# A hybrid encoder trunk in fp32 on one core: one merged form for all residual norms, layer 0's adaLN on TensorE, and a new order in the attention's tail

## The chip, the cores and the metric

One core of a Trainium2 chip. The metric is the device time of one execution in microseconds. The engines are TensorE (PE), VectorE (DVE), ScalarE (ACT), GpSimd (POOL) and SyncE (SP), which issues the DMAs.

## What is computed

The sequence has 512 positions of 1024 channels. Layer 0 mixes with a diagonal state space (S5) that ends in a GLU, layer 1 with differential attention; each is followed by a gated FFN with a short convolution. Around every sub-layer stands the same frame, with shift, scale and gate from a conditioning vector (adaLN):

```python
mod = cond @ ada_w[i] + ada_b[i]
sh_t, sc_t, g_t, sh_c, sc_c, g_c = jnp.split(mod, 6, axis=-1)
h = modulate(rms_norm(x, norm_g[i, 0]), sh_t, sc_t)
h = s5_mixer(h, ...)        # or diff_attention(h, ...)
x = x + g_t[:, None, :] * rms_norm(h, norm_g[i, 1])
h = modulate(rms_norm(x, norm_g[i, 2]), sh_c, sc_c)
h = conv_ffn(h, ffn_w_in[i], ffn_conv_w[i], ffn_conv_b[i], ffn_w_out[i])
x = x + g_c[:, None, :] * rms_norm(h, norm_g[i, 3])
```

So between two sub-layers stand two root mean squares: that of the sub-layer's output y, and that of the new x.

## The kernel before

All engines run hand-written programs tied by semaphores. Activations lie transposed, channels on partitions: x is 8 tiles of 128 channels by 512 positions (`f` counts tiles). Weights come in units of 1 MB (128 x 2048) through two buffers `raw`; ACT makes the high part `whi`, DVE the low part `wlo` (`split_high`, `split_low`), and a product is three matmuls per step, high by high, high by low, low by high (`gemm_step`, L1738 to L1740). A unit has 16 steps: two output tiles (halves) of eight `k`.

**adaLN.** `ada_w` comes as 48 units of 1 MB. Of layer 0 the first third (8 units) is made by PE in the start-up (`ada_unit`, L1615: four matmuls of one column by 512 a unit, all to partition 0), copied by ACT to one row and turned into a column by PE (L1636). The other 40 units are summed by DVE (`ada_step`, L1250) beside the GLU (two a unit) and the first FFN (two in each of the first twelve units), and PE turns the sums with ones (`reduce_acc`, L1622).

**Start-up.** DVE makes the S5 matrices (`complex_rows`), PE transposes them (L1646), DVE normalises u, PE spreads its modulation (L1650, for which DVE waits before `output_powers`, L1100 to L1105), and four pieces of scan and Toeplitz products (L1679) follow.

**The merge.** Behind the GLU DVE and PE work in two rounds (`first_norms`, `statistic`): squares of y, root, y times gate times root, x plus that; then squares of the new x, root, and the next input with high and low part. Behind FFN 0 and behind the output projection they use one round (`tile_sums`, `both_roots`, `next_input(r)`, `barrier(r)`, r = 1, 2): for each tile, when it is ready, the sums of y*y, x*y*gate and (y*gate)^2 are added, and the new x's mean square follows from these and the old one, which is kept in `stat[:, 24:28]`. PE keeps itself busy there with idle products (L1778). DVE writes the new input tile by tile, and the first FFN unit follows it.

**Attention's tail.** Each head is done in four query blocks: scores (L1937), row maximum, exponentials, `combine` (L1492), `turn` (L1953), `weigh` (L1962). PE does these for a head while it does projection steps of another (`attend`, whose `fill` gives some steps at two places per block). The last two heads are filled by the first two units of the output projection (`early_output`, `wo_step`). Behind the last weighing stand `head_norm` on DVE, `turn_out` (L1971), the low part of the last head on POOL, and the rest of the projection; its third unit has its own buffers `wx`.

## Time and profile before

| what | value |
|---|---|
| median of 3 runs | 1386.8 us (1385.84 to 1389.02) |
| profiled execution | 1383.9 us |
| its span | 1382.1 us |
| PE busy | 1235.3 us (89%) |
| DVE, ACT, POOL busy | 860.7, 497.8, 430.3 us |
| chain that ended last | PE 75%, DVE 16%, issue 3%, DMA 2% |

The page gives the share of each engine and the span in slices. Busy time says little by itself: what counts is which wait ends last in a stage. The timeline lists instructions in order, with the idle time before them and what ended it in brackets. A float32 matmul shows as two records, a float32r one as one.

### The profile page before, as it was taken

What the parts mean: (1) busy time and instruction counts of PE and PEld (TensorE: products, weight loads), DVE (VectorE), ACT (ScalarE), POOL (GpSimd) and SP (SyncE); (2) the same over time, 40 slices, a digit from 0 to 9 for tenths busy, and PEclk for the clock granted to TensorE, in tenths of its full rate; (3) what the DMA queues carried; (4) which work ended last, traced back from release to release, by engine and by line L of the source; (5) the groups of instructions that cost most, each with busy time, mean ns of one, the idle gap of its engine ahead of it and who ended that gap; (6) DMA issues with size and microseconds to landing.
All of it is one profiled execution on the core that took longest, in us unless ns stands there. A gap on an engine that the chain in (4) does not pass through costs nothing.

```text
span 1382.1 us, 17492 instructions
## 1 busy us (share of the span) xinstructions
PE 1235.3 (89%) x6312; PEld 994.6 (72%) x6312; DVE 860.7 (62%) x1107; ACT 497.8 (36%) x749; POOL 430.3 (31%) x274
## 2 busy tenths in 40 slices
PE   5532599988999999999999999887999999999995
PEld 0222588876888888888878776666778888887884
DVE  8999878747989744424295468775964444443323
ACT  3052342224433433414233254544544434342311
POOL 3993011123554534300020443530133344431001
PEclk9766799958999999999999999999999999999998
DMA  8001988802767513233222332220122222323211
GB/s 343 1 1 25 167 265 309 299 31 74 291 245 289 196 64 110 101 104 110 92 73 92 92 92 62 75 77 32 61 92 91 91 91 98 114 92 110 104 61 61
DMA packets 35430, 164.97 MB, mean 119 GB/s; under 512 B 4528, under 2 KB 14000, under 8 KB 17200
## 3 DMA queue, kind: packets, MB, share of 16 engines
q1 hardware_dynamic: 34368, 163.97, 35.0%
q8 instruction: 35, 0.57, 0.2%
q10 hardware_dynamic: 1008, 0.27, 0.1%
q14 instruction: 19, 0.16, 0.0%
HBM read 156.95 MB, written 3.08 MB: 116 GB/s over the span
## 4 chain that ended last, share of the span: by engine, by line
PE 75%; DVE 16%; issue 3%; DMA 2%; ACT 1%; SPq 1%; POOL 1%; DVEq 0%; ACTq 0%; POOLq 0%
PE psum L1738 16%; PE psum L1739 16%; PE psum L1740 16%; PE psum L1879 5%; PE psum L1880 5%; PE psum L1881 5%; PE psum L1622 2%; PE psum L1962 1%; PE psum L1937 1%; PE psum L1823 1%; SPq L375 1%; PE psum L1922 1%; PE psum L1923 1%; PE psum L1924 1%; DVE ca L1103 1%
## 5 line engine op out<-in xcount | busy, mean ns | idle before, releaser
L1738 PE MATMUL psum<-hhi,whi 128*128 128x512 f32 x960 | 382.4, 398 | 3.9 <-DVE hlo L1309 2.7
L1739 PE MATMUL psum<-hlo,whi 128*128 128x512 f32 x960 | 376.8, 393 | 0.0
L1740 PE MATMUL psum<-hhi,wlo 128*128 128x512 f32 x960 | 376.7, 392 | 0.0
L1187 DVE TENSOR_TENSOR wlo<-raw,whi 128x2048 fp32r<-128x2048 f32 x82 | 199.0, 2427 | 169.6 <-ACT whi L693 169.6
L693 ACT ACTIVATE whi<-raw 128x2048 fp32r<-128x2048 f32 x81 | 155.1, 1915 | 178.1 <-PE psum L1881 146.1
L567 POOL TENSOR_TENSOR ca<-ca,cb 128x512 f32<-128x512 f32 x44 | 138.6, 3151 | 247.2 <-ACT ca L803 247.2
L1738 PEld LDWEIGHTS psum<-hhi,whi 128*128 128x128 f32 x960 | 182.0, 190 | 45.6 <-issue 5.5
L1740 PEld LDWEIGHTS psum<-hhi,wlo 128*128 128x128 f32 x960 | 181.9, 189 | 38.6
L1739 PEld LDWEIGHTS psum<-hlo,whi 128*128 128x128 f32 x960 | 182.1, 190 | 36.2
L1403 DVE SCALAR_TENSOR_TENSOR ca<-psum,convp,ca 128x511 f32<-128x511 f32 x44 | 32.9, 749 | 200.0 <-ACT ca L799 199.9
L1879 PE MATMUL psum<-ghi,whi 128*128 128x512 f32 x352 | 137.2, 390 | 1.5 <-DVE wlo L1187 1.5
L1880 PE MATMUL psum<-glo,whi 128*128 128x512 f32 x352 | 137.0, 389 | 0.0
L1881 PE MATMUL psum<-ghi,wlo 128*128 128x512 f32 x352 | 136.9, 389 | 0.0
L553 POOL TENSOR_TENSOR x<-x,y_late 128x512 f32<-128x512 f32 x17 | 22.9, 1351 | 293.2 <-DVE y_late L1366 172.0
L1250 DVE SCALAR_TENSOR_TENSOR ada_acc<-ada_ring,cond,ada_acc 128x2048 f32<-128x2048 f32 x40 | 106.1, 2652 | 3.0 <-DMA ada_ring<-in_ada_w 2.8
L799 ACT ACTIVATE ca<-psum,convp 128x512 f32<-128x512 f32 x44 | 34.2, 778 | 134.3 <-PE psum L1740 133.8
L569 POOL TENSOR_TENSOR glo<-ca,ghi 128x512 f32 x44 | 69.6, 1583 | 41.5 <-ACT ghi L805 41.5
L805 ACT ACTIVATE ghi<-ca 128x512 f32 (+1 forms) x44 | 27.8, 633 | 151.7 <-POOL ca L567 151.7
L1879 PEld LDWEIGHTS psum<-ghi,whi 128*128 128x128 f32 x352 | 66.1, 188 | 16.1 <-DVE wlo L1187 2.4
L1880 PEld LDWEIGHTS psum<-glo,whi 128*128 128x128 f32 x352 | 66.1, 188 | 13.7
L1881 PEld LDWEIGHTS psum<-ghi,wlo 128*128 128x128 f32 x352 | 66.1, 188 | 13.7
L873 ACT ACTIVATE prob<-psum,stat 128x128 f32<-128x128 f32 (+3 forms) x64 | 33.2, 523 | 75.9 <-DVE stat L1477 75.9
(344 smaller groups left out, 1736.0 us busy)
## 6 DMA issues: line engine op xcount, KB each, us to landing
raw<-in_units SPq DMA_DIRECT2D x92, 1024.0 KB, 4.8
ada_ring<-in_ada_w SPq DMA_DIRECT2D x40, 1024.0 KB, 4.8
ada_raw<-in_ada_w SPq DMA_DIRECT2D x8, 1024.0 KB, 14.9
toep<-toeplitz_rows SPq DMA_DIRECT2D x32, 128.0 KB, 8.6
qk_sw<-ca SPq DMA_DIRECT2D x32, 128.0 KB, 2.3
u<-in_x_blocks SPq DMA_DIRECT2D x1, 2048.0 KB, 14.1
x<-in_x_t SPq DMA_DIRECT2D x1, 2048.0 KB, 8.3
out_t<-x SPq DMA_DIRECT2D x8, 256.0 KB, 2.0
```

What stands on the lines that cost most here:

```text
L567: nc.gpsimd.tensor_tensor(ca[:, s, :], ca[:, s, :], cb[:, s, :], ALU.mult).then_inc(g_ready, 1)
L569: nc.gpsimd.tensor_tensor(glo[:, j, :], ca[:, s, :], ghi[:, j, :].bitcast(F32), ALU.subtract).then_inc(g_lo, 1)
L693: A(whi[:, s, :], raw[:, s, :], ACT.Copy).then_inc(split_hi, 1)
L799: A(dst[:, s, :], psum[:, 2 * s + i, :], ACT.Identity, scale=convp[:, layer, j, i, 2:3], bias=convp[:, layer, j, i, 3:4]).then_inc(tap2, 1)
L1187: TT(wlo[:, s, :], raw[:, s, :], whi[:, s, :].bitcast(F32), ALU.subtract).then_inc(split_lo, 1)
L1250: STT(ada_acc[:, slot, :], ada_ring[:, e, :], cond[:, 1, bass.ds(k[0], 1)], ada_acc[:, slot, :], ALU.mult, ALU.add).then_inc(ada_added, 1)
L1738: M(out, w_hi, hi[:, k, :], start=(k == 0), stop=False)
L1739: M(out, w_hi, lo[:, k, :], start=False, stop=False)
L1740: return M(out, w_lo, hi[:, k, :], start=False, stop=(k == KT - 1))
L1879: M(out, whi[:, s, w], ghi[:, row, :], start=(fixed and row == 0), stop=False)
L1880: M(out, whi[:, s, w], glo[:, row, :], start=False, stop=False)
L1881: return M(out, wlo[:, s, w], ghi[:, row, :], start=False, stop=(fixed and row == JT - 1))
```

## The change

It does three things.

1. The merge behind the GLU takes the form of the later two, as r = 0. The squares of x are made by ACT (`x_square`) and added by DVE (`x_square_add`) in the first four GLU units; PE sums them ahead of unit 7. Each GLU tile's sums are made in its unit (`glu_squares`, `tile_sums(0, f)`). The next unit's second buffer is split in halves, as it was behind the projection. POOL adds seven of the eight residual tiles instead of three.
2. The second and third third of layer 0's adaLN (16 units) move from DVE to PE's start-up, through two buffers; each unit's four matmuls now write partitions 0, 32, 64, 96 of one bank. The 24 units of layer 1 stay on DVE: one in each GLU unit, one or two in each of the first twelve FFN units.
3. In the tail the early projection steps are given out in halves, by counts per place, and eight of the third unit's sixteen steps go behind the last weighing.

```diff
-N_ADA_PE = KT
+N_ADA_PE = 3 * KT
...
-        POOL_X = ((1, 3, 5), tuple(range(1, KT)), tuple(range(1, KT)), (1, 3, 5))
+        POOL_X = 3 * (tuple(range(1, KT)),) + ((1, 3, 5),)
...
+            eng.wait_ge(h_low, KT * r + f + 1)
+        def ada0_slot(n):
+            return n % N_ADA0 if n < KT else n % 2
+        def ada0_count(n):
+            return 16 * (n // N_ADA0 + 1 if n < KT else (n - KT) // 2 + 3)
...
-                wait(sp, ada_used, n + 1 - N_ADA0)
-                sp.dma_start(ada0_raw[:, n % N_ADA0, :], a["ada_w"][n]).then_inc(ada0_landed[n % N_ADA0], 16)
+                wait(sp, ada_used, n + 1 - N_ADA0 if n < KT else n - 2 if n < KT + 2 else n - 1)
+                slot = ada0_slot(n)
+                sp.dma_start(ada0_raw[:, slot, :], a["ada_w"][n]).then_inc(ada0_landed[slot], 16)

...
+            load_unit(2, 0, None)
+            load_unit(3, 1, None)
+            def load_one(i, s, half):
+                load_ada(i + 2, s)
+                load_unit(i + 4, s, half)
+                load_ada(2 * i - 10, 0)
+                load_ada(2 * i - 9, 1)
+            pairs(sp, 0, N_GLU + 4, load_one)
+            pairs(sp, N_GLU + 4, N_GLU + 8, load_both)
+            for i in range(N_GLU + 8, N_GLU + 10):
+                load_ada(i + 6, i % 2)
+                load_unit(i + 4, i % 2, None)
...
+            def copy_row(third):
+
+                act.wait_ge(ada_used, KT * third + KT)
+                if third == 2:
+                    act.wait_ge(mod0_psum, 1)
+                for b in range(4):
+                    ins = A(sq[32 * b:32 * b + 1, third % 2, :], psum[32 * b:32 * b + 1, third % 2, :], ACT.Copy)
+                ins.then_inc(row_copied, 1)
+
...
+            def x_square(f):
+
+                act.wait_ge(x_in, 16)
+                wait(act, xsq_added, f - 2 if f > 2 else 0)
+                A(x_sq[:, f % 2, :] if f else x_sum[:], x[:, f, :], ACT.Square).then_inc(xsq_ready, 1)
+
+            def glu_squares(f):
+
+                y, g = y_glu[:, f, :], gate[:, 0, f:f + 1]
+                act.wait_ge(y_ready, f + 1)
+                wait(act, sum_a, f - 2 if f > 2 else 0)
+                A(sq[:, f % 2, :] if f else ssum[:], y, ACT.Square).then_inc(sqa_ready, 1)
+                wait(act, sum_c, f - 2 if f > 2 else 0)
+                A(glu_sq[:, f % 2, :] if f else cb[:, 1, :], y, ACT.Square, scale=g).then_inc(sqc_ready, 1)
+                act.wait_ge(sqc_ready, f + 1)
+                A(y, y, ACT.Copy, scale=g).then_inc(yg_ready, 1)
+
...
+            dve.wait_ge(mod_psum, 2)
+            modulation(0, (2, 3, 4, 5))
+            signal(mod_read)
...
+                    pairs(dve, 0, 4, partial(body, first=lambda j, s, half: ada_step(
+                        j + KT, s, half + KT // 2 + 1, j, 1)))
+                    dve.wait_ge(acc_clear, 3)
+                    pairs(dve, 4, 8, partial(
+                        body, first=lambda j, s, half: ada_step(2 * j + (KT - 4), 0, j + 3, j, 1),
+                        second=lambda j, s, half: ada_step(2 * j + (KT - 3), 1, j + 3, j - 4, 0)))
+                    pairs(dve, 8, 12, partial(body, first=lambda j, s, half: ada_step(
+                        j + (KT + 4), s, half + 7, j - 4, 0)))
...
+            def glu(i, s):
+                dve.wait_ge(sig_ready, i + 1)
+                TT(y_glu[:, i, :], psum[:, 2 * s, :], ca[:, s, :], ALU.mult).then_inc(y_ready, 1)
+                if i < N_GLU - 1:
+                    split_low(i + 2, s, None)
+                    if i < KT // 2:
+                        if i:
+                            x_square_add(2 * i)
+                        x_square_add(2 * i + 1)
+                    ada_step(i, s, i // 2 + 1, i, 0)
+                tile_sums(0, i)
+
+            for i in range(N_GLU - 1):
+                glu(i, i % 2)
+            first_half_low(0)
+            ada_step(N_GLU - 1, 1, 4, N_GLU - 1, 0)
+            glu(N_GLU - 1, 1)
+            next_input(0, {KT - 1: lambda: second_half_low(0)})
...
-            def ada_unit(k, s):
-
-                pe.wait_ge(ada0_landed[s], 16 * (k // N_ADA0) + 16)
+            def ada_unit(n):
+
+                third, k = divmod(n, KT)
+                pe.wait_ge(ada0_landed[ada0_slot(n)], ada0_count(n))
+                if k == 0:
+                    wait(pe, row_copied, third - 1)
-                    ins = M(psum[0:1, b, :], cond[:, 1, k:k + 1], ada0_raw[:, s, 512 * b:512 * b + 512],
+                    ins = M(psum[32 * b:32 * b + 1, third % 2, :], cond[:, 1, k:k + 1],
+                            ada0_raw[:, ada0_slot(n), 512 * b:512 * b + 512],
+
+            def turn_row(third):
+
+                pe.wait_ge(row_copied, third + 1)
+                if third:
+                    pe.wait_ge(mod_psum if third > 1 else mod0_psum, 1)
+                for b in range(4):
+                    rows = slice(32 * b, 32 * b + 1)
+                    for q in range(4):
+                        f = THIRD * third + 4 * b + q
+                        ins = M(psum[:, 7, f:f + 1], sq[rows, third % 2, P * q:P * q + P], ones[rows, 0:1],
+                                start=True, stop=True)
+                    if b < 3:
+                        ins.then_inc(row_turned, 1)
+                        pe.wait_ge(row_turned, 3 * third + b + 1)
+                ins.then_inc(mod_psum if third else mod0_psum, 1)
...
+                if t % 2:
+                    ada_unit(2 * KT + t // 2)
             pe.wait_ge(umod_rhs, 2)
...
+            pairs(pe, 2, N_GLU - 2, glu)
+            glu(N_GLU - 2, 0, None)
+            pe.wait_ge(xsq_added, KT - 1)
+            for t in range(QT):
+                ins = M(psum[:, 5, t:t + 1], x_sum[:, P * t:P * t + P], col[:, 0:1],
+                        start=True, stop=True)
+            ins.then_inc(stat_x, 1)
+            pe.wait_ge(y_ready, N_GLU - 2)
+            pe.wait_ge(split_lo, N_GLU)
+            for step in range(2 * KT):
+                ins = gemm_step(1, step, hhi, hlo)
+                if step == KT - 1:
+                    ins.then_inc(glu_half, 1)
+            ins.then_inc(unit_done, 1)
...
-            def early_output(steps_):
-
-                for m, k in steps_:
-                    if k == 0:
-                        pe.wait_ge(split_lo, U_WO + m + 1)
-                        pe.wait_ge(raw_copied, 2 * (HEADS - 1 + m))
-                    wo_step(m, k)
+            def early_output(steps_, counts):
+
+                todo = iter([(m, k, half) for m, k in steps_ for half in range(2)])
+                for count in counts:
+                    for m, k, half in itertools.islice(todo, count):
+                        if k == 0 and half == 0:
+                            pe.wait_ge(split_lo, U_WO + m + 1)
+                            pe.wait_ge(raw_copied, 2 * (HEADS - 1 + m))
+                        wo_step(m, k, half)
...
-            attend(HEADS - 2, 0, early_output([(0, k) for k in range(5)]))
-            attend(HEADS - 1, 1, early_output([(1, k) for k in range(5)] + [(0, 5), (1, 5)]))
+            attend(HEADS - 2, 0, early_output([(0, k) for k in range(5)], (1, 1, 1, 1, 1, 1, 2, 2)))
+            attend(HEADS - 1, 1, early_output([(1, k) for k in range(5)] + [(0, 5), (1, 5)],
+                                              (1, 1, 2, 2, 2, 2, 2, 2)))
             turn(HEADS - 1, 3)
             weigh(HEADS - 1, 3)
+            pe.wait_ge(split_lo, U_WO + 3)
+            pe.wait_ge(exp_done, 8 * HEADS)
+            for k in range(KT // 2):
+                for half in range(2):
+                    wo_step(2, k, half)
             turn_out(HEADS - 1)
 
             for m in range(2):
-                wo_step(m, KT - 2)
+                for half in range(2):
+                    wo_step(m, KT - 2, half)
             for m in range(2):
-                pe.wait_ge(ot_lo, KT + 2)
-                gemm_step(m, KT - 1, ohi, olo).then_inc(y_tile, 1)
-                gemm_step(m, 2 * KT - 1, ohi, olo).then_inc(unit_done, 1)
-            for m in range(2, N_WO):
-                pe.wait_ge(split_lo, U_WO + m + 1)
-                if m == 3:
-                    pe.wait_ge(sqc_ready, KT + 2)
-                w = (4, wx[:, 0], wx[:, 1]) if m == 2 else (0, None, None)
-                for step in range(2 * KT):
-                    ins = gemm_step(1, step, ohi, olo, *w)
-                    if step == KT - 1:
-                        ins.then_inc(y_tile, 1)
-                ins.then_inc(unit_done, 1)
+                wo_step(m, KT - 1, 0).then_inc(y_tile, 1)
+                wo_step(m, KT - 1, 1).then_inc(unit_done, 1)
+            for half in range(2):
+                for k in range(KT // 2, KT):
+                    ins = wo_step(2, k, half)
+                ins.then_inc(unit_done if half else y_tile, 1)
+            pe.wait_ge(split_lo, U_WO + 4)
+            pe.wait_ge(sqc_ready, 2 * KT + 2)
+            for step in range(2 * KT):
+                ins = gemm_step(1, step, ohi, olo, 0)
+                if step == KT - 1:
+                    ins.then_inc(y_tile, 1)
+            ins.then_inc(unit_done, 1)
```

The order of `ada_w` in memory (`_ada_units`) follows the new order of use.

PE in the start-up, around the transposes of `lb`. Before:

```order
L1615 MATMUL psum<-ada_raw,cond 1x512 [waits ada0_landed1]
L1615 MATMUL psum<-ada_raw,cond 1x512 x3
L1615 MATMUL psum<-ada_raw,cond 1x512 [waits ada0_landed2]
L1615 MATMUL psum<-ada_raw,cond 1x512 x3
L1636 MATMUL psum<-ones,mod_row 128x1 [waits row_copied]
L1636 MATMUL psum<-ones,mod_row 128x1 x15
L1646 MATMUL psum<-ident,lb_re 128x128 [waits row0_ready,lb_dve,lb_pool]
L1646 MATMUL psum<-ident,lb_re 128x128 x7
```

Now (unit 15 of `ada_raw`, the transposes, units 16 and 17):

```order
L1585 MATMUL psum<-ada_raw,cond 1x512 x3
L1631 MATMUL psum<-ident,lb_re 128x128 [waits row0_ready,lb_dve,lb_pool]
L1631 MATMUL psum<-ident,lb_re 128x128 x7
L1585 MATMUL psum<-ada_raw,cond 1x512 [waits row_copied,ada0_landed0]
L1585 MATMUL psum<-ada_raw,cond 1x512 x3
L1631 MATMUL psum<-ident,lb_re 128x128 [waits inb_ready]
L1631 MATMUL psum<-ident,lb_re 128x128 x3
L1631 MATMUL psum<-ident,lb_re 128x128 [waits inb_ready]
L1631 MATMUL psum<-ident,lb_re 128x128 x3
L1585 MATMUL psum<-ada_raw,cond 1x512 [waits ada0_landed1]
L1585 MATMUL psum<-ada_raw,cond 1x512 x3
L1631 MATMUL psum<-ident,lb_re 128x128 [waits inb_ready]
```

Units 8 to 15 stand ahead of the first transpose, and of the other eight one behind every eight transposes, each with the wait for its load.

DVE in the GLU, the last two units before the merge. Before:

```order
L1263 TENSOR_TENSOR y_glu<-psum,ca 128x512 [waits sig_ready]
L1250 SCALAR_TENSOR_TENSOR ada_acc<-ada_ring,cond,ada_acc 128x2048 [waits ada_added,ada_landed0]
L1187 TENSOR_TENSOR wlo<-raw,whi 128x2048 [waits split_hi]
L1250 SCALAR_TENSOR_TENSOR ada_acc<-ada_ring,cond,ada_acc 128x2048 [waits ada_added,ada_landed1]
L1263 TENSOR_TENSOR y_glu<-psum,ca 128x512 [waits sig_ready]
```

Now, the third unit from product to sums:

```order
L1400 TENSOR_TENSOR y_glu<-psum,ca 128x512 [waits sig_ready]
L1179 TENSOR_TENSOR wlo<-raw,whi 128x2048 [waits split_hi]
L1252 TENSOR_TENSOR x_sum<-x_sum,x_sq 128x512 [waits xsq_added,xsq_ready] x2
L1242 SCALAR_TENSOR_TENSOR ada_acc<-ada_ring,cond,ada_acc 128x2048 [waits ada_added,ada_landed0]
L1269 TENSOR_TENSOR ssum<-ssum,sq 128x512 [waits sum_a,sqa_ready]
L1279 TENSOR_TENSOR on<-x,y_glu 128x512 [waits sum_b,yg_ready]
L1280 TENSOR_TENSOR cb<-cb,on 128x512 [waits dve_step]
L1283 TENSOR_TENSOR cb<-cb,glu_sq 128x512 [waits sum_c,sqc_ready]
```

One adaLN sum is gone; two sums of x's squares and the four passes of the tile's sums are new.

PE in the tail, from the last head's fourth `turn` on. Before:

```order
L1953 MATMUL psum<-ident,att 128x128 [waits ot_copied,attt_copied,att_ready]
L1953 MATMUL psum<-ident,att 128x128 x3
L1962 MATMUL psum<-v_sb,att_t 128x128 [waits attt_copied]
L1962 MATMUL psum<-v_sb,att_t 128x128 x3
L1971 MATMUL psum<-ident,on 128x128 [waits attt_copied,on_ready]
L1971 MATMUL psum<-ident,on 128x128 x3
L1738 MATMUL psum<-ohi,whi 128x512 [waits ot_lo]
L1739 MATMUL psum<-olo,whi 128x512
L1740 MATMUL psum<-ohi,wlo 128x512
```

Now:

```order
L1921 MATMUL psum<-ident,att 128x128 [waits ot_copied,attt_copied,att_ready]
L1921 MATMUL psum<-ident,att 128x128 x3
L1930 MATMUL psum<-v_sb,att_t 128x128 [waits attt_copied]
L1930 MATMUL psum<-v_sb,att_t 128x128 x3
L1729 MATMUL psum<-ohi,wx 128x512 [waits ot_lo,exp_done,split_lo]
L1730 MATMUL psum<-olo,wx 128x512
L1731 MATMUL psum<-ohi,wx 128x512
L1729 MATMUL psum<-ohi,wx 128x512 [waits ot_lo]
L1730 MATMUL psum<-olo,wx 128x512
L1731 MATMUL psum<-ohi,wx 128x512
L1729 MATMUL psum<-ohi,wx 128x512 [waits ot_lo]
L1730 MATMUL psum<-olo,wx 128x512
```

Four of the eight steps on `wx` are seen; the other four follow, and then the four transposes of `turn_out` (L1939) that stood directly behind the weighing.

## Rows read from the trace of the kernel before

**Rows 1.** The page, part 2: granted clock in 40 slices of 34.6 us, in tenths

```profile
PEclk9766799958999999999999999999999999999998
```

**Rows 2.** Stretches: us, busy PE, PEld, DVE, ACT, POOL, then PEclk, DMA share, GB/s

```profile
187.00:276.00 89.00, 89.00 (x412) 73.77 (x408) 66.24 (x36) 24.98 (x28) 15.11 (x9) 1.00 0.82 309
276.00:317.00 41.00, 31.36 (x149) 28.12 (x147) 17.64 (x51) 9.37 (x14) 8.50 (x5) 0.54 0.07 29
```

**Rows 3.** Timeline, PE and ACT, 275 to 353: start us, length us, engine, line, tiles

```profile
275.91 3.63 PE L1622 MATMUL psum<-ones,ada_acc 128*128 128x1 f32 x32
...
295.63 13.81 PE L1823 MATMUL psum<-col,sq 128*128 128x1 f32 x64 [4.16 <-ACT sq L728]
...
317.36 0.77 PE L1738 MATMUL psum<-hhi,whi 128*128 128x512 f32 x1 [2.67 <-DVE hlo L1309]
...
352.15 0.78 ACT L799 ACTIVATE ca<-psum,convp 128x512 f32<-128x512 f32 x1 [0.63 <-PE psum L1740]
```

**Rows 4.** Timeline of the merge behind the projection, PE, DVE and ACT

```profile
984.72 1.75 PE L1778 MATMUL psum<-whi 128*128 128x512 f32 x7
...
1001.81 0.47 PE L1738 MATMUL psum<-hhi,whi 128*128 128x512 f32 x1 [0.70 <-DVE hlo L1375]
...
988.45 0.69 DVE L1344 TENSOR_TENSOR cb<-cb,ca 128x512 f32<-128x512 f32 x1
...
1036.08 0.78 ACT L799 ACTIVATE ca<-psum,convp 128x512 f32<-128x512 f32 x1 [2.19 <-PE psum L1740]
```

**Rows 5.** Timeline of PE in the start-up; last, a stretch with 32-column groups

```profile
39.34 7.03 PE L1615 MATMUL psum<-ada_raw,cond 128*1 128x512 f32 x16
...
48.32 4.61 PE L1636 MATMUL psum<-ones,mod_row 1*128 1x1 f32 x32 [1.96 <-ACT mod_row L662]
...
66.29 6.76 PE L1646 MATMUL psum<-ident,lb_re 128*128 128x128 f32 x32 [13.36 <-issue]
...
91.79 0.80 PE L1650 MATMUL psum<-ca,sel 128*128 128x128 f32 x2 [13.37 <-DVE ca L1164]
...
116.00:119.00 3.00, 2.73 (x104) 2.74 (x108) 2.79 (x6) 0.00 (x0) 0.00 (x0) 0.50 0.00 0
```

**Rows 6.** DMA of the adaLN tile, a stretch of it, DVE and POOL, first Toeplitz matmul

```profile
DMA to landing us min/median/max: 4.7/14.9/19.7
...
24.00:34.00 10.00, 10.00 (x21) 1.86 (x20) 9.72 (x8) 4.56 (x8) 8.64 (x7) 0.85 1.01 422
...
92.63 1.76 DVE L1100 TENSOR_TENSOR cl_re<-pw_re,bc_par 128x512 f32<-128x512 f32 x1 [0.89 <-PE psum L1650]
...
127.17 0.69 DVE L1105 TENSOR_TENSOR cl_im<-cl_im,ca 128x512 f32<-128x512 f32 x1
...
110.53 1.70 POOL L487 TENSOR_TENSOR cl_im<-cl_im,cb 128x512 f32<-128x512 f32 x1
...
146.37 3.68 PE L1679 MATMUL psum<-toep,u 128*64 128x128 f32 x32 [12.13 <-DMA toep<-toeplitz_rows]
```

**Rows 7.** Timeline of the attention's tail, PE, then DVE's first row behind it

```profile
921.84 0.90 PE L1953 MATMUL psum<-ident,att 128*128 128x128 f32 x3 [2.67 <-DVE att L1492]
...
924.83 1.65 PE L1962 MATMUL psum<-v_sb,att_t 128*128 128x128 f32 x6 [2.09 <-ACT att_t L884]
...
945.80 0.94 PE L1962 MATMUL psum<-v_sb,att_t 128*128 128x128 f32 x6 [1.27 <-ACT att_t L884]
...
955.31 1.11 PE L1971 MATMUL psum<-ident,on 128*128 128x128 f32 x4 [4.51 <-DVE on L1520]
...
962.96 0.39 PE L1738 MATMUL psum<-ohi,wx 128*128 128x512 f32 x1
...
965.17 2.29 DVE L1187 TENSOR_TENSOR wlo<-raw,whi 128x2048 fp32r<-128x2048 f32 x1 [9.92 <-ACT whi L693]
```

**Rows 8.** Timeline of DVE in the GLU's seventh unit

```profile
266.46 2.34 DVE L1250 SCALAR_TENSOR_TENSOR ada_acc<-ada_ring,cond,ada_acc 128x2048 f32<-128x2048 f32 x1
...
268.72 3.38 DVE L1187 TENSOR_TENSOR wlo<-raw,whi 128x2048 fp32r<-128x2048 f32 x1
```

395 lines of the change are left out of this document (136 added, 259 removed).

## The prediction

> **What bounds the kernel now.** I read the page first: the clock granted to TensorE (PE) is full almost everywhere, and low in the first eighth of the span and in one slice near 300 us (each digit is 34.6 us) [rows 1]. The view by stretches says why. In the eight GLU units PE has no gap at all and VectorE (DVE) is busy for 66 of 89 us; in the 41 us behind them PE does almost no useful work at a clock of 0.54 [rows 2]. So in the GLU only PE's own work counts, and between the GLU and the first FFN the time hangs on a chain of small steps. In order of time that chain is: the last adaLN sums turned by ones (L1622), the root of y's mean square, then the squares of x after the residual, one tile at a time through PE (13.8 us for 64 matmuls), a second root, and only then the first FFN step at 317.36 [rows 3]. The kernel has the same task at two later places in another form, the merged one; behind the output projection it goes from PE's last step at 984.72 to the first FFN step at 1001.81 [rows 4]. The start-up is a chain of DVE work that PE and DMA wait for [rows 5, 6], and in the attention's tail PE waits for DVE and ScalarE (ACT) [rows 7].
>
> **Part 1, the merge between GLU and FFN 0.** I compare one point that both forms have: the FFN's third unit is finished when ACT starts its L799. Before, that is 352.15, or 76.2 us behind PE's last GLU step at 275.91 [rows 3]. In the merged form behind the projection it is 1036.08 - 984.72 = 51.4 us [rows 4]. Both hold three units of 11 us (eight of them fill the 89 us of the GLU [rows 2]). In the new code one reduction of 16 small matmuls (3.6 us, the first of rows 3) stands before the third unit and one fewer behind it, so it counts here and comes back there. I add what is worse here than there. Behind the projection DVE's sums end 4.4 us after PE's last step (988.45 + 0.69) [rows 4]. Here the last tile needs a sigmoid and a product first, then three ACT passes and four DVE passes of about 0.7 us; and ahead of them on DVE stand the half split of the next unit and the last adaLN sum of 2.34 us [rows 8], which begin some 9.8 us into a unit of 11 us and so hold the product up by about 0.7 us. Nine passes of 0.69 us with a small copy are 6.3 us (an estimate from the length of L1344), with the late product 7.0 us, so 2.6 us more than 4.4. The x statistic that PE now does ahead of unit 7 is 8 records, 0.11 us each in the first row of rows 3, about 1.0 us of PE. So 76.2 - 51.4 - 2.6 - 1.0 = **21.2 us** gained. Bounds: 19, if that tail comes another 2 us late, as long as one adaLN sum; 24.8, the bare difference.
>
> What this moves into the GLU is hidden while a unit's DVE work stays under PE's 11 us: product 0.7, split 2.3, one adaLN sum 2.34 instead of two, up to two sums of x's squares 1.4, four tile sums 2.7, together 9.4 us. If the cover goes, each excess us is paid in up to four units. POOL loses its six sums per statistic there and gets four more residual tiles, in the same rhythm as at the later merges. SyncE loads 2 MB instead of 3 MB in a GLU unit.
>
> **Part 2, sixteen adaLN units move to the start-up.** Before, the eight units there end on PE at 46.4, PE then stands idle until the transposes at 66.29 and again until 91.79, when DVE has its right-hand side [rows 5]. Now units 8 to 15 come before the transposes and 16 to 23 between them, and the matmul at 91.79 comes after all of them. DVE waits for it before it makes the output powers. Price of a unit on PE: two took 7.03 us at the high clock, 3.5 us each [rows 5]. But each unit's four matmuls now write partitions 0, 32, 64 and 96, so four column groups. The kernel has such work: at a granted clock of 0.50, 104 records of 64 columns in 32-column groups took 2.73 us, 26 ns each, where the transposes, one after another and for most of their time at the low clock, took 6.76 us for 32 records of 128 columns, 106 ns per 64 columns [rows 5]. Four groups overlap fourfold. So a unit is 7.0 / 4 = 1.75 us at the low clock, 0.9 at the high one. Units 8 and up have only two buffers, and a load lands 4.7 us after its issue at best [rows 6]. A pair of units hence costs 4.7 + 1.75 + 0.3 = 6.7 us. Unit 7 ends by its load: 11 MB at 422 GB/s [rows 6] from 5.5 us on are 33 us, with latency and its own matmuls I let it end at 38, the row's copy and turn at 46 (before they ended at 52.9, 6.5 us behind unit 7 [rows 5]), the first pair (landed by then) at 49.4, and seven more pairs at 96.3. The matmul of 91.79 is **4.6 us late**. Its follower is the DVE row at 92.63, 36 passes up to 127.9, of which those beside POOL take 1.5 to 1.8 us and those after POOL's end at 112.2 take 0.69 [rows 6]. A delay pushes passes out of POOL's company, so it costs 0.69 / 1.5 of itself: **+2.1 us**. Bounds: 0 (DVE has no right-hand side before 91.79) and the serial price, below. The two later turns of rows (4.6 us each, as the first one took) stand before the first state matmuls, which DVE reads only after its output powers, at 127.9; the modulation's seven short DVE passes ahead of the scan end long before PE has its Toeplitz tiles at 146.37 [rows 6]. Both cost nothing while those tiles are late.
>
> The Trainium skill (TensorEngine Tiling (Array Packing), Tiling Modes) says that a change of tiling mode drains TensorE, which speaks against units put between transposes. [...]
>
> **Part 3, the attention's tail.** Two edits. (a) The ten early projection steps of the last head but one stood 4, 4, 2, 0 in the four query blocks and now stand 2, 2, 2, 4; of the last head 4, 4, 4, 2 become 2, 4, 4, 4. A step is three matmuls, 0.69 us (11 us for 16). The places that gain steps are those where PE waited 2.67, 2.09 and 1.27 us [rows 7]. The places that lose them are where PE was behind: at most six steps, 4.1 us, and 0.7 us on the matmuls of 924.83 that ran at the low clock. DVE and POOL run beside each other there and will not let all of it through: I take **3.0** between 0 and 5. (b) Eight steps of the third unit go behind the last weighing, 5.5 us of PE work in a wait of 4.5 us [rows 7]; the transposes at 955.31 start 1.0 us late but at the high clock, and the last low part (POOL) comes about as late as before or 0.5 us later, and the two units' last four steps (2.7 us) follow it. The start of the third unit's rest, 962.96 before, comes 0.6 us earlier. What it does not bring is the 5 us of work taken out: from there DVE works without idling, from 965.17 to the end of its sums at 989.1 [rows 4, 7], because the split of the fourth unit may start only when the first two units are done. PE's remaining work behind 962.96 falls from 21.8 to 16.4 us and PE then waits. So part 3 is worth **3.6 us**, between 1 and 6. PE's longer wait may leave the low clock for the merge behind it, 0 to 1 us, which lies inside these bounds.
>
> **Sum.** The profiled execution took 1383.9 us. 1383.9 - 21.2 + 2.1 - 3.6 = 1361.2. The median of the three runs stands 2.9 us above the profiled execution, so I forecast **1364 us**. One measurement of this kernel can tell about 0.2%, 2.8 us.
>
> **Rivals.**
> - *The tail gives nothing* (13%). For it: DVE and POOL, not PE, set the last head but one from its third block on. Against: PE rows without idling in both heads' first blocks. Time 1364 + 3.6 = 1368.
> - *The GLU becomes DVE's* (10%). 9.4 of 11 us is close, a split beside POOL took 3.4 instead of 2.3 us [rows 8], and the tile sums wait for ACT passes queued behind its split. One us over in five units: 1369. Against: POOL is idle there now.
> - *The tail is PE's* (4%): then (b) brings its 4.9 us, 1359.
> - *Column groups do not overlap, at the high clock* (7%). A unit is 3.5 us, a pair 8.5 us; two groups of transposes add 0.9 us per unit, so the matmul of 91.79 comes at about 122. Of 30 us DVE gets back 12 (36 passes at 0.69 are 25 us instead of 35), so +18 instead of +2.1: 1380.
> - *The same at the low clock* (3%), the case on the other side. 7 us a unit, 8.5 us with transposes: 46 + 56 + 68 = 170, 78 us late, 12 got back: 1364 + 64 = 1428, slower. It turns slower than before once that matmul comes later than about 130 (22.7 us of gain and 12 given back, plus the 2.1 and 4.6 in the forecast). Against: the 26 ns record.
> - My forecast has 63%.
>
> **How the numbers follow.** The low end takes merge 24.8, tail 6 and start-up 0, together 1356. The high end takes merge 19, tail 1 and start-up +5, together 1372, and 1374 with one or two us of GLU excess; I close at 1373. That leaves out the two overlap cases, a tenth. Range 1356 to 1373. Faster by over 0.2%: all but the last case, and a remainder for an unseen wait, 0.95; within 0.2%, 0.01; slower 0.04.
>
> **What would show it.** Right: PE's last GLU step to the FFN's first step about 19 us; the FFN's third unit done about 54 us behind it; the matmul before the output powers at 92 to 98; records of the adaLN units near 0.21 us apart at the low clock; DVE without idling between its split for the fourth unit and the sums' end, PE idle some 6 us before the merge behind the projection. Wrong: adaLN records 0.43 us apart or more, DVE gaps in the tail, PE waits for y or for a low part within the GLU.

## The result and the profile after

The changed kernel takes **1363.6 us** (median of 4 runs, 1361.96 to 1365.41), the kernel before 1387.45 beside it: ratio 0.983, 95% interval 0.981 to 0.985, so 1.7% faster. The forecast was 1364 between 1356 and 1373. The total came as forecast; the stages came only in part as forecast.

The profiled execution of after is the one of 1365.41 us, its span 1363.6 (before 1382.1). Read by stages, both from their traces:

| stretch (PE's clock time) | before | after | change | forecast |
|---|---|---|---|---|
| start to the first GLU step | 187.84 | 193.47 | +5.6 | +2.1 |
| GLU, to its last step | 88.07 | 89.02 | +0.95 | +1.0 |
| last GLU step to the statistic behind FFN 0 | 422.3 | 398.2 | -24.1 | -22.2 |
| from there to the scores of head 6 (the last but one) | 206.3 | 205.3 | -1.0 | 0 |
| to the first new input tile behind the projection | 93.9 | 93.8 | -0.1 | -3.6 |
| to the end | 383.7 | 383.7 | 0 | 0 |

The stages add up to -18.5 us, where the medians differ by 23.9 and the forecast by 22.7. The profiled execution of before was 3.5 us faster than its median and that of after 1.8 us slower than its own, so this table shows 5.3 us less than the runs do. Part may lie in the start-up: in a second profile of the old one (experiment 3) it took 191.16 us, 3.3 more than in the table.

The page of after, part 2, granted clock (beside [rows 1]):

```profile
PEclk9585889988999999999999999989799999999997
```

Two stretches of after, GLU and merge, in the columns of [rows 2]:

```profile
193.00:282.00 89.00, 89.00 (x408) 73.82 (x405) 61.03 (x60) 39.56 (x51) 3.57 (x2) 1.00 0.52 200
282.00:301.00 19.00, 15.84 (x62) 11.85 (x60) 15.62 (x44) 6.16 (x11) 3.14 (x3) 0.82 0.29 115
```

PE has no gap in the GLU, as before. The 41 us behind it have become 19. The timeline of PE and ACT there (beside [rows 3]):

```profile
282.49 1.75 PE L1776 MATMUL psum<-whi 128*128 128x512 f32 x7
285.81 1.05 PE L1785 MATMUL psum<-col,ssum 128*128 128x1 f32 x8 [1.58 <-DVE ssum L1269]
301.14 0.47 PE L1729 MATMUL psum<-hhi,whi 128*128 128x512 f32 x1 [0.69 <-DVE hlo L1318]
323.23 4.34 PE L1609 MATMUL psum<-ones,ada_acc 128*128 128x1 f32 x32
341.42 0.78 ACT L788 ACTIVATE ca<-psum,convp 128x512 f32<-128x512 f32 x1 [5.32 <-PE psum L1731]
```

From the last GLU step (282.49) to the first FFN step 18.65 us, to the third unit's end 58.9. From the first FFN step to the third unit's end it takes 40.3 us, where the merge behind the projection had 34.3 [rows 4]; the reduction at 323.23 (4.34 us) is only a part of this. DVE's rows ahead of the third unit in after, and then PE at the third unit behind the projection in the kernel before:

```profile
321.58 2.35 DVE L1242 SCALAR_TENSOR_TENSOR ada_acc<-ada_ring,cond,ada_acc 128x2048 f32<-128x2048 f32 x1
323.83 3.36 DVE L1179 TENSOR_TENSOR wlo<-raw,whi 128x2048 fp32r<-128x2048 f32 x1
```

```profile
1024.58 0.50 PE L1738 MATMUL psum<-hhi,whi 128*128 128x512 f32 x1 [0.53 <-DVE wlo L1187]
```

The third unit's low part is ready at 327.19, 4 us after PE's second unit ended (323.23). An adaLN sum of 2.35 us stands ahead of it, and the low part takes 3.36 us beside passes of POOL, where behind the projection it took 2.28 with no sum ahead.

The start-up (beside [rows 5, 6]): PE, then DVE's first and last output power, then the first and third piece's Toeplitz matmuls.

```profile
40.77 7.62 PE L1599 MATMUL psum<-ones,sq 1*128 1x1 f32 x32 [2.55 <-ACT sq L647]
...
71.63 1.89 PE L1585 MATMUL psum<-ada_raw,cond 128*1 128x512 f32 x8 [1.21 <-DMA ada_raw<-in_ada_w]
...
91.07 1.04 PE L1585 MATMUL psum<-ada_raw,cond 128*1 128x512 f32 x8 [0.40 <-DMA ada_raw<-in_ada_w]
92.04 1.09 PE L1631 MATMUL psum<-ident,lb_im 128*128 128x128 f32 x8
...
97.90 0.49 PE L1637 MATMUL psum<-ca,sel 128*128 128x128 f32 x2
...
98.42 1.64 DVE L1089 TENSOR_TENSOR cl_re<-pw_re,bc_par 128x512 f32<-128x512 f32 x1 [6.58 <-PE psum L1637]
...
128.58 0.68 DVE L1094 TENSOR_TENSOR cl_im<-cl_im,ca 128x512 f32<-128x512 f32 x1
...
146.81 3.68 PE L1670 MATMUL psum<-toep,u 128*64 128x128 f32 x32 [9.15 <-DMA toep<-toeplitz_rows]
...
178.34 3.68 PE L1670 MATMUL psum<-toep,u 128*64 128x128 f32 x32 [9.89 <-DMA toep<-toeplitz_rows]
```

An adaLN unit (8 records) takes 1.89 us at the low clock and 1.04 at the high one. The turn of the first row (40.77) took 7.62 us at a granted clock of 0.50; before it took 4.61 at 0.78, behind adaLN units that had kept PE busy at 1.00. The matmul at 97.90 is 6.1 us late, but DVE's last output power ends at 129.26, only 1.4 late, and the first Toeplitz matmul 0.4. The third one is 5.2 late (before 173.10).

The tail (beside [rows 4, 7]); the last line is the statistic of the same merge in the kernel before:

```profile
898.27 0.44 PE L1921 MATMUL psum<-ident,att 128*128 128x128 f32 x2 [2.98 <-DVE att L1466]
...
901.83 2.08 PE L1905 MATMUL psum<-qk 64*128 64x512 f32 x4
...
936.86 0.60 PE L1939 MATMUL psum<-ident,on 128*128 128x128 f32 x4
...
945.37 2.29 DVE L1179 TENSOR_TENSOR wlo<-raw,whi 128x2048 fp32r<-128x2048 f32 x1 [9.38 <-ACT whi L683]
...
967.45 1.87 PE L1785 MATMUL psum<-col,ssum 128*128 128x1 f32 x8 [5.93 <-DVE ssum L1269]
```

```profile
987.26 1.05 PE L1787 MATMUL psum<-col,ssum 128*128 128x1 f32 x8 [0.79 <-DVE ssum L1331]
```

PE no longer waits for the head's norm at the transposes (936.86). But it now waits 2.98 us in the third block of head 6; the scores behind it (901.83) take 2.08 us, those of head 7 at full clock 1.13, and the statistic at 967.45 takes 1.87 where it took 1.05 before. Both stand behind a wait of PE and run at the low clock.

### The profile page after: what moved, and what is told of

It reads as the page before. It is cut to its first block, busy times and chain, and to the rows that moved or that the text cites. A ratio compares the mean times of both kernels' runs of the same rounds, so it can differ in the third digit from the quotient of the medians.

```text
span 1363.6 us, 17638 instructions
## 1 busy us (share of the span) xinstructions
PE 1242.1 (91%) x6423; PEld 990.0 (73%) x6423; DVE 828.6 (61%) x1131; ACT 510.1 (37%) x777; POOL 417.4 (31%) x265
## 4 chain that ended last, share of the span: by engine, by line
PE 75%; DVE 13%; DMA 4%; issue 3%; ACT 2%; SPq 1%; DVEq 0%; POOL 0%; ACTq 0%; POOLq 0%
PE psum L1729 16%; PE psum L1731 15%; PE psum L1730 15%; PE psum L1850 5%; PE psum L1852 5%; PE psum L1851 5%; DMA ada_raw<-in_ada_w 3%; SPq L373 1%; PE psum L1930 1%; PE psum L1905 1%; PE psum L1585 1%; PE psum L1890 1%; PE psum L1892 1%; PE psum L1891 1%; DMA toep<-toeplitz_rows 1%
## 5 line engine op out<-in xcount | busy, mean ns | idle before, releaser
L1179 DVE TENSOR_TENSOR wlo<-raw,whi 128x2048 fp32r<-128x2048 f32 x81 | 189.2, 2336 | 177.2 <-ACT whi L683 177.2
L552 POOL TENSOR_TENSOR ca<-ca,cb 128x512 f32<-128x512 f32 x44 | 152.9, 3476 | 239.6 <-ACT ca L792 239.6
L794 ACT ACTIVATE ghi<-ca 128x512 f32 (+1 forms) x44 | 27.8, 632 | 165.8 <-POOL ca L552 165.8
L554 POOL TENSOR_TENSOR glo<-ca,ghi 128x512 f32 (+1 forms) x44 | 63.3, 1440 | 41.3 <-ACT ghi L794 41.3
L1585 PE MATMUL psum<-ada_raw,cond 128*1 128x512 f32 x192 | 38.1, 889 | 38.2 <-DMA ada_raw<-in_ada_w 38.2
```

Source lines behind the costliest of these rows:

```text
L552: nc.gpsimd.tensor_tensor(ca[:, s, :], ca[:, s, :], cb[:, s, :], ALU.mult).then_inc(g_ready, 1)
L554: nc.gpsimd.tensor_tensor(glo[:, j, :], ca[:, s, :], ghi[:, j, :].bitcast(F32), ALU.subtract).then_inc(g_lo, 1)
L1179: TT(wlo[:, s, :], raw[:, s, :], whi[:, s, :].bitcast(F32), ALU.subtract).then_inc(split_lo, 1)
L1585: ins = M(psum[32 * b:32 * b + 1, third % 2, :], cond[:, 1, k:k + 1], ada0_raw[:, ada0_slot(n), 512 * b:512 * b + 512], start=(k == 0), st ...
```

## The experiments

Each is the changed kernel with the edit shown, cut down to its main lines (`...` marks a cut), unless said otherwise; the ratio is to the kernel before, run beside it (for the changed kernel 0.983).

**1. The old tail in the changed kernel** (both parts undone).

```diff
-            attend(HEADS - 2, 0, early_output([(0, k) for k in range(5)], (1, 1, 1, 1, 1, 1, 2, 2)))
+            attend(HEADS - 2, 0, early_output([(0, k) for k in range(5)], (2, 2, 2, 2, 2)))
...
-                                              (1, 1, 2, 2, 2, 2, 2, 2)))
+                                              (2, 2, 2, 2, 2, 2, 2)))
...
-            for k in range(KT // 2):
-                for half in range(2):
-                    wo_step(2, k, half)
             turn_out(HEADS - 1)
...
-                for k in range(KT // 2, KT):
+                for k in range(KT):
```

> The changed kernel with the attention's tail as it was (steps in pairs, the whole third projection unit behind the transpose of the last head). Theory A (the prediction's part 3): the tail's edit is worth 3.6 us, so this comes to about 1367. Theory B (what the trace of the changed kernel suggests: from the scores of the last head but one to the end it takes 477.56 us, before 477.61): the edit gave nothing, so this comes to 1363 to 1364. From scores(6,0) to the fourth unit's split on DVE it should take 1.35 us more than in the changed kernel in both; what comes behind must tell. The start-up is left as changed: if the third Toeplitz load lands again about 14 us behind its issue (178 us), the change causes it; if nearer 11.5 us (173 us), it is chance.

1368.55 us, ratio 0.986 (0.984 to 0.988). **2. The new counts alone**, the third unit whole behind the transposes (the last two pieces of that diff):

> The changed kernel with the halves given out by the new counts, but the third projection unit whole behind the transpose of the last head. Theory A: the counts are worth 3.0 and the move 0.6, so this is 0.6 us slower than the changed kernel. Theory B: behind the last weighing DVE sets the end (the sums of the projection's tiles take 26.2 us without a gap), so the moved half is worth nothing: within 0.3 us of the changed kernel in the stretch from scores(6,0) to the last sum.

1363.21 us, ratio 0.9825 (0.980 to 0.985). On one chip the counts are worth 5.3 us, and the moved half nothing that can be seen. Up to the end of DVE's sums the tail is as long with it as without (85.14 us without, below), and behind them the first new tile comes after 9.9 to 10.5 us with it and after 9.3 without: with the half moved PE waits 5.9 us ahead of its statistic and runs it at the low clock (1.87 us), without it waits 0.8 us (1.05). **3. The new tail in the kernel before** (the same lines put there):

> The kernel before with the tail's edit alone (halves by the new counts, half of the third unit behind the last weighing). Theory A (what the run with the old tail now suggests): the edit is worth 3 to 5 us, by the third unit's half that fills PE's wait for the head's norm; so 0.4% faster than the kernel before in the runs, and the stretch from the scores of the last head but one to the sums' end is 81 to 83 us, before 84.65. Theory B: that kernel's tail shows a shorter stretch at the low clock than the others by chance, and the edit gives 1 us or less. It also gives the old start-up a second time: if the third Toeplitz load again lets local(2) begin 26.7 us behind local(0), the 28.1 to 31.5 us of the changed kernels are the change's; if 28 to 30, chance.

1384.38 us, ratio 0.998 (0.997 to 0.999): 2.8 us, between 1.1 and 4.6. So the edit is worth 3 to 5 us; theory A stands in size (its cause, the moved half, does not, by experiment 2), although the two profiles of before and after show no difference. Why they don't is in the granted clock. The stretch from the scores of head 6 to the end of DVE's sums in six kernels (before; after; the old tail; the counts alone; the new tail in the kernel before; experiment 4), in the columns of [rows 2]:

```profile
904.49:989.14 84.65, 70.43 (x361) 56.41 (x361) 58.79 (x113) 43.53 (x88) 13.73 (x10) 0.92 0.21 69
```

```profile
886.04:969.33 83.29, 70.73 (x357) 54.71 (x357) 58.86 (x112) 43.55 (x88) 12.78 (x10) 0.93 0.21 70
```

```profile
886.33:974.80 88.47, 74.42 (x361) 58.77 (x360) 58.44 (x113) 43.55 (x88) 12.76 (x10) 0.86 0.20 66
```

```profile
886.24:971.38 85.14, 73.02 (x361) 56.88 (x360) 58.84 (x113) 43.39 (x88) 12.72 (x10) 0.90 0.20 69
```

```profile
907.65:988.74 81.09, 68.70 (x357) 52.91 (x356) 59.17 (x112) 43.39 (x88) 13.74 (x10) 0.97 0.22 72
```

```profile
886.70:967.71 81.01, 76.34 (x398) 59.59 (x397) 58.80 (x113) 43.38 (x88) 12.79 (x10) 1.00 0.21 72
```

DVE's busy time is the same in all (58.4 to 59.2 us), the length follows the clock: the old tail took 84.65 at 0.92 and 88.47 at 0.86, the new one 83.29 at 0.93 and 81.09 at 0.97. One profile of each kernel would have told a tale of its own. With the new tail it was 84.5 to 85.3 us at 0.92 in five more profiles (experiments 5 to 9).

So the old tail and the new one are both 2 to 4 us shorter in the kernel before than in the changed one. Part of this can be seen in the third block of head 6. First POOL and PE in experiment 3, where the new tail stands in the kernel before, then DVE in the changed kernel:

```profile
916.87 3.66 POOL L603 TENSOR_TENSOR qk_sw<-qk_sw,sinb 128x512 f32<-128x512 f32 x2 [1.09 <-DMA qk_sw<-ca]
...
917.23 0.44 PE L1954 MATMUL psum<-ident,att 128*128 128x128 f32 x2 [0.36 <-DVE att L1493]
```

```profile
894.26 1.21 DVE L1482 TENSOR_SCALAR nwt<-nwt 128x4 int32<-128x4 int32 x1
...
896.85 1.36 DVE L1466 SCALAR_TENSOR_TENSOR att<-prob,stat 128x256 f32<-128x256 f32 x1
```

In the kernel before and in experiment 3 POOL waits 1.1 us for a DMA there. In this pause DVE's last small pass takes 0.17 us and its `att` 0.48, and PE then waits 0 or 0.36 us. In ten of the twelve profiles of the changed kernel and its variants POOL does not pause, and in the other two only 0.48 us. Without the pause the same two DVE passes take 1.2 and 1.4 us beside POOL. PE waits 1.1 us there with the old tail and 2.3 to 3.0 with the new one (without idle products). Why the DMA lands later in the one base than in the other is open.

**4. PE kept busy where it waits in the tail.**

```diff
+            attend(HEADS - 2, 0, early_output([(0, k) for k in range(5)], (1, 1, 1, 1, 1, 1, 2, 2), {4: 8, 5: 3}))
...
+                    if place in idle:
+                        pe.wait_ge(raw_copied, 2 * HEADS)
+                        idle_products(idle[place], 3)
...
-                    idle_products(7, 7)
+                    idle_products((7, 7, 33)[r], 7)
```

> The changed kernel with eight and three idle products more in the third query block of the last head but one, where PE waits 2.98 and 1.27 us and its clock falls to 0.50 behind, and 33 instead of 7 ahead of the merge behind the projection, where PE waits 5.93 us and its three statistics take 1.85 us instead of 1.05. Theory: PE's waiting is what lowers the clock, and the low clock is what moves the tail's time between runs; so the granted clock stays at 1.00 there, the scores of the fourth block take 1.1 instead of 2.08 us, the statistics 1.05; from the scores of head 6 to those of head 7 22.0 us instead of 23.46, from the sums' end to the first t 8.5 instead of 10.5: 3 to 3.5 us in all, 1360. Rival: the clock falls for another reason (the small matmuls of the attention), stays at 0.50 in these stretches, and the idle products delay PE: 1364 or more.

1362.51 us, ratio 0.981 (0.979 to 0.984): 1 to 2 us, less than foreseen and within the noise of the runs. The trace shows the mechanism where it was aimed. PE in the third and fourth block of head 6:

```profile
895.79 1.99 PE L1776 MATMUL psum<-whi 128*128 128x512 f32 x8
...
898.97 0.44 PE L1921 MATMUL psum<-ident,att 128*128 128x128 f32 x2 [1.19 <-DVE att L1466]
...
902.02 1.13 PE L1905 MATMUL psum<-qk 64*128 64x512 f32 x4
```

The scores take 1.13 us instead of 2.08, the clock of the stretch is 1.00, and head 6 takes 21.1 us (886.70 to 907.81) instead of 23.5. Head 6 took 21.0 to 21.1 us in all three profiles with these idle products, and 23.1 to 23.9 in the eight profiles of the changed kernel and its variants with the new counts and without them. In experiment 3 it took 21.1 us without any, but there PE waited only 0.36 us. So in this stage it is PE's wait that is followed by the low clock, and idle products in it hold the clock. Ahead of the merge the 33 products kept the first two statistics at 1.05 us, but the third took 1.80: the clock fell behind two rows of one-column matmuls, though PE had had no wait longer than 0.27 us.

**5. All adaLN matmuls in one column group.**

```diff
-                    ins = M(psum[32 * b:32 * b + 1, third % 2, :], cond[:, 1, k:k + 1],
+                    ins = M(psum[0:1, third % 2, :], cond[:, 1, k:k + 1],
                             ada0_raw[:, ada0_slot(n), 512 * b:512 * b + 512],
-                            start=(k == 0), stop=(k == KT - 1))
+                            start=True, stop=True)
```

(ACT's `copy_row` reads partition 0 four times. The sum over the eight units of a third is left out, the work is the same.)

> The changed kernel with the four matmuls of each adaLN unit on the same output partition 0 instead of 0, 32, 64 and 96 (each product starts and stops by itself and layer 0's adaLN comes out wrong; the work is the same). Theory: the change to four column groups is what makes a unit 1.9 us at the low clock and 1.0 at the high one; on one group it is 3.5 (the 7.03 for two of before) and 1.75, the interleaved units delay the u modulation's matmul to about 110 us and the first GLU step by 8 to 12 us: 1372 to 1376 in all. Rival: the units are bound by their DMA (3.2 us each) and the groups buy little: the matmul comes at most 3 us later, below 1366.

1384.41 us, ratio 0.998 (0.996 to 1.000): 21 us more, all but 3 of the change's gain. Its trace, the last interleaved unit, the matmul behind it, the second turn of a row, and DVE's first and last output power:

```profile
123.26 3.59 PE L1585 MATMUL psum<-ada_raw,cond 128*1 128x512 f32 x8
126.78 0.49 PE L1637 MATMUL psum<-ca,sel 128*128 128x128 f32 x2
127.20 4.37 PE L1599 MATMUL psum<-ones,sq 1*128 1x1 f32 x32
...
127.31 0.69 DVE L1089 TENSOR_TENSOR cl_re<-pw_re,bc_par 128x512 f32<-128x512 f32 x1 [35.54 <-PE psum L1637]
...
149.91 0.69 DVE L1094 TENSOR_TENSOR cl_im<-cl_im,ca 128x512 f32<-128x512 f32 x1
```

A unit is 3.59 us instead of 1.04: four column groups do overlap, 3.5-fold. What I wrote just before the run was too small; the prediction's rival for this case had the matmul at 122 and +16 us over the forecast, where 126.8 and +21 came. Of the 34.7 us of delay DVE gave back 12.0, as that rival said. The turn of a row, in four row groups with a wait between them, took 4.37 us here at a granted clock of 1.00.

**6. Five buffers for units 8 to 15. 7. In addition the first two GLU units loaded while the DMA queues are empty.**

```diff
-            return n % N_ADA0 if n < KT else n % 2
+            return n % N_ADA0 if n < 2 * KT else (n + 1) % 2
...
+            sp.wait_ge(ada_used, N_ADA_PE)
+            for n in range(2):
+                sp.dma_start(raw[:, n, :], a["units"][n]).then_inc(raw_landed[n], 16)
             store_rows(0)
```

(The first line is experiment 6, with its counts; the others, moved up from behind `load_toeplitz(1)`, are 7.)

> The changed kernel with five buffers instead of two for adaLN's units 8 to 15 too (16 to 23 stay with two). Theory: in the changed kernel units 10 to 15 wait 1.2 to 3.1 us each for their DMA, which puts the u modulation's matmul at 97.9 us instead of 91.8. With five buffers that matmul is back at 92 to 93 us; since DVE's passes cost 1.5 us beside POOL and 0.7 alone, DVE's end moves by 1.4 us only, so 1361.5 to 1362.5 in all. Rival: the DMA rate limits (24 MB by then), the units wait as before and the time is that of the changed kernel, 1363.6.

> The changed kernel with five buffers for adaLN's units 8 to 15, and the first two GLU weight units loaded ahead of the Toeplitz rows' store (where the DMA queues are empty from about 98 to 131 us) instead of between the second and the third Toeplitz load. Theory: the Toeplitz loads run at 115 to 130 GB/s (8 to 9 us a piece), and the 2 MB of weights take 5 us of that queue, so PE's local(2) waits for the sum; with the weights gone local(2) comes 4 to 5 us earlier and the first GLU step with it: 1358 to 1359.5, against 1363.2 with the five buffers alone. Rival: with the weights gone the next piece is bound by DVE's scans, which are busy without a gap there; then the first GLU step comes 1 to 2 us earlier only.

6: 1363.22 us, ratio 0.982 (0.980 to 0.9845), equal to experiment 2 on the same chip. 7: 1360.51, ratio 0.980 (0.979 to 0.982). PE's rows in 6, then in 7:

```profile
91.92 0.49 PE L1637 MATMUL psum<-ca,sel 128*128 128x128 f32 x2 [1.26 <-DVE ca L1153]
...
174.75 3.68 PE L1670 MATMUL psum<-toep,u 128*64 128x128 f32 x32 [8.56 <-DMA toep<-toeplitz_rows]
```

```profile
168.55 1.97 PE L1670 MATMUL psum<-toep,u 128*64 128x128 f32 x32 [0.40 <-DMA toep<-toeplitz_rows]
...
176.16 3.25 PE L1682 MATMUL psum<-cl_re,hx 64*64 64x128 f32 x28 [4.26 <-issue]
```

The matmul is back where it was (91.79), so two buffers had made it late. DVE's output powers end at 127.96 instead of 129.26; the runs show no gain beyond their noise. With the weights out of the Toeplitz loads' way PE's wait of 8.56 us falls to 0.40, and PE then waits for DVE's work on the scans, which has no gap from 166 to 183 us: the first GLU step comes at 189.06, 1.2 us before experiment 6 (190.23). The rival was right on this: DVE is close behind. The medians differ by 2.7 us, but their intervals overlap.

**8. A second, useless low-part pass on DVE in GLU units two to four.**

```diff
+                    if 0 < i < 4:
+                        dve.wait_ge(split_hi, i + 3)
+                        link(TT(wlo[:, s, :], raw[:, s, :], whi[:, s, :].bitcast(F32), ALU.subtract))
                     split_low(i + 2, s, None)
```

> The changed kernel with the low part of the weights made twice in the second, third and fourth GLU unit (2.3 us more of DVE in each, same result). It measures how far DVE is from being the bound there. Theory (the forecast's side): DVE idles 1.7 of 10.95 us in these units and the two buffers of weights take up part of a delay, so PE waits for 0 to 2 us in all: 1363.4 to 1365.4. Rival (the GLU is already at DVE's bound, and each us more of DVE is one of PE): 3 x 2.3 = 6.9 us more, 1370.

1364.95 us, ratio 0.984 (0.982 to 0.9855), and in the trace the GLU takes 89.18 us from its first step to the end of its last, exactly as in the changed kernel, without a wait of PE. 2.3 us more in three units cost nothing: DVE's work in the GLU is well inside PE's time.

**9. The reductions in FFN 0 spread**, one matmul ahead of each step of the unit behind.

```diff
-                        reduce_acc(slot, THIRD * (3 + third))
-                        pairs(pe, lo, hi, body)
+                        body(lo, 0, None, partial(reduce_step, slot, THIRD * (3 + third)))
+                        body(lo + 1, 1, None)
+                        if lo + 2 < hi:
+                            pairs(pe, lo + 2, hi, body)
```

> The changed kernel with the three reductions of layer 1's adaLN in the first FFN given out one matmul ahead of each of the sixteen steps of a unit, instead of sixteen in a row between two units. In the changed kernel the unit that follows a reduction comes 16.2 us behind the last one, the others 10.87: 5.4 us for a reduction whose matmuls take 3.5 at the high clock, with a granted clock of 0.5 to 0.6 in the 4 us behind it. Theory: the row of one-column matmuls lowers the clock, and that is 1 to 2 us of each; spread, the clock stays at 1.00 and a reduction costs 3.5, so 3 to 6 us in all: 1358 to 1360.5. Rival: the clock has nothing to do with it (a reduction costs 5.4 because the next unit's weights load late), then the cost stays: 1363.4.

1364.11 us, ratio 0.984 (0.982 to 0.9855): no gain. Three views say why. In the changed kernel, ACT's follower of units 10 and 11 with the second reduction between them, and the clock in the 4 us behind that reduction:

```profile
417.49 0.78 ACT L788 ACTIVATE ca<-psum,convp 128x512 f32<-128x512 f32 x1 [0.24 <-PE psum L1731]
433.72 0.78 ACT L788 ACTIVATE ca<-psum,convp 128x512 f32<-128x512 f32 x1 [6.20 <-PE psum L1731]
...
421.00:425.00 4.00, 4.00 (x12) 3.09 (x11) 4.00 (x3) 0.25 (x1) 3.58 (x1) 0.57 0.17 31
```

In the spread kernel the same two rows and, before them in time, PE at the third unit:

```profile
325.30 0.35 PE L1608 MATMUL psum<-ones,ada_acc 128*128 128x1 f32 x2 [3.95 <-DVE wlo L1179]
...
418.23 0.78 ACT L788 ACTIVATE ca<-psum,convp 128x512 f32<-128x512 f32 x1 [0.24 <-PE psum L1731]
432.99 0.78 ACT L788 ACTIVATE ca<-psum,convp 128x512 f32<-128x512 f32 x1 [6.94 <-PE psum L1731]
```

Between two units without a reduction the step is 10.8 to 10.95 us. So the second reduction costs 14.76 - 10.87 = 3.9 us spread and 5.4 in a row, and spread the granted clock is 1.00 in the same 4 us: the theory holds for it. But the first one had covered a wait of 3.95 us of PE for the third unit's low part, which DVE makes late behind an adaLN sum. Spread, the wait is open, and from the first FFN step to the third unit it takes 43.1 us instead of 40.3. The one takes what the others give.

**10. The fourth projection unit split early**, into the memory of the values, which the last weighing has read.

```diff
             copy_output(HEADS - 1)
+            act.wait_ge(raw_landed[1], 16 * (U_WO // 2 + 2))
+            A(wv[:, 0, :], raw[:, 1, :], ACT.Copy).then_inc(split_hi, 1)
...
-            split_high(U_WO + 3, 1, U_WO // 2 + 1)
...
-            split_low(U_WO + 3, 1, None)
+            dve.wait_ge(split_hi, U_WO + 4)
+            TT(wv[:, 1, :], raw[:, 1, :], wv[:, 0, :].bitcast(F32), ALU.subtract).then_inc(split_lo, 1)
...
-                ins = gemm_step(1, step, ohi, olo, 0)
+                ins = gemm_step(1, step, ohi, olo, 0, wv[:, 0], wv[:, 1])
```

> The changed kernel with the fourth projection unit split into the memory of the values, which is free behind the last weighing: ACT makes its high part at 933 and DVE its low part in the 9.4 us in which it idles, instead of 945.4. Theory: from there to the sums' end DVE is the bound (26.2 us without a gap), so its 2.29 us go: the sums end 23.9 us behind the end of the first two units instead of 26.2, and the time is 1361.3. Rival: PE or ACT is close behind (the projection's last tile), then less than 1 us.

1357.65 us, ratio 0.9775 (0.976 to 0.979): 6 to 7 us, the best single edit. ACT and DVE, then PE:

```profile
932.76 1.92 ACT L937 ACTIVATE wv<-raw 128x2048 fp32r<-128x2048 f32 x1
...
936.13 2.28 DVE L1556 TENSOR_TENSOR wv<-raw,wv 128x2048 fp32r<-128x2048 f32 x1
943.36 0.69 DVE L1278 TENSOR_TENSOR cb<-x,y_late 128x512 f32<-128x512 f32 x1 [4.95 <-ACT y_late L761]
...
963.70 1.05 PE L1788 MATMUL psum<-col,ssum 128*128 128x1 f32 x8 [1.60 <-DVE ssum L1271]
```

ACT's 1.92 us stood on the same chain as DVE's 2.29 (ACT makes the squares behind it), together 4.2 us: from the transposes to the sums' end it takes 27.8 us instead of 32.5, where 2.3 less had been foreseen. And PE's wait ahead of the merge shrinks from 5.93 to 1.60 us, so the statistics run at the high clock: from the sums' end to the first new tile 8.1 instead of 10.5.

**11. and 12. Together**: experiments 4 (its first part), 7, 9 and 10 in one kernel; then the same with the first reduction in a row again and 13 idle products ahead of the merges.

> The edits that the runs so far favour, in one kernel: five buffers for adaLN's units 8 to 15 and the first two GLU units loaded in the idle DMA stretch (3 us by the runs), the fourth projection unit split early into the values' memory (6 us), eight and three idle products in the third block of the last head but one (1 to 2 us), the reductions spread (3 to 6 us by the theory of the run beside). Theory: they lie in different stages and add up: 1346 to 1350. Rival: the idle products and the early split work on the same clock, and a part is had only once: 1350 to 1353.

> The kernel of all favoured edits, with the first reduction of layer 1's adaLN again sixteen matmuls in a row (the trace of the spread one shows that it covers a wait of 3.95 us for the third unit's low part, which is open where it is spread) and 13 instead of 7 idle products ahead of the merges behind the GLU and the projection, where PE still waits 1.6 us. Theory: the wait is covered again (3 to 3.9 us), and the six more products fill the 1.6 us in front of the statistics; if they keep the clock at 1.00 there, up to 1 us at each merge: 1347 to 1350 in all. Rival: the statistics' own one-column matmuls lower the clock whatever stands ahead of them (they stayed at 0.50 behind 33 products in one run), then 1349 to 1350, from the reduction alone.

11: 1352.49 us, ratio 0.975 (0.974 to 0.9765), behind its theory's 1346 to 1350; the exposed wait of experiment 9 is in it (323.54, 3.95 us). 12: **1349.75 us**, ratio 0.973 (0.971 to 0.975), faster than both kernels. The intervals of 11 and 12 overlap, and what of the step comes from the reduction and what from the idle products was not run apart. PE at its merge behind the projection:

```profile
951.95 3.11 PE L1781 MATMUL psum<-whi 128*128 128x512 f32 x13
955.33 1.05 PE L1790 MATMUL psum<-col,ssum 128*128 128x1 f32 x8 [0.27 <-DVE ssum L1271]
```

## Why the prediction was right, and where it was not

- **Merge (-21.2 with the statistic).** The merged form brought its gain in place: 18.65 us to the first FFN step (about 19 said; the last tile's passes cost 1.6 us more than behind the projection, 2.6 said), the x statistic 0.94 us (1.0). Up to the statistic behind FFN 0 it brought 24.1 - 0.95 = 23.1. The failing step is "one reduction of 16 small matmuls (3.6 us, the first of rows 3) stands before the third unit and one fewer behind it, so it counts here and comes back there". It was wrong at both ends.
  - Before the third unit the comparison with the projection's merge left out what stands on DVE only here, an adaLN sum and POOL's passes: the low part comes 4 us late, and with it the third unit was done 58.9 us behind the GLU, not 54.0 + 3.6 = 57.6. The reduction fills this wait; spread out of it, the wait is open (3.95 us, experiment 9), so without any reduction the unit would be done near 57.6 us (61.5 there, less 3.9 for the spread reduction) and not at the 54 said.
  - Behind the third unit 6.8 us came back (346.1 to 339.3), not 3.6: a reduction in a row costs 5.4 us, because the clock falls behind it (experiment 9), and the last of the three in the kernel before cost 7.0 us (17.79 us from unit to unit, 10.8 without). I priced the row of small matmuls by its length alone.
  - That the two errors, 1.3 us lost and 3.2 gained, went against each other is luck.
- **GLU.** The DVE rival (10%) is refuted: no wait of PE, and experiment 8 finds the slack.
- **Start-up (+2.1).** The mechanism held, several sizes did not. The column groups overlap as read from the 26 ns record (1.89 and 1.04 us a unit, 1.75 and 0.9 said), and experiment 5 shows that the change hangs on it.
  - The matmul came 6.1 us late, not 4.6. The row's turn is what was mis-sized: it ended at 48.4, not 46, because it ran at a granted clock of 0.50 (7.62 us; 6.43 at 0.62 in experiment 6, 4.37 at 1.00 in experiment 5). The units before it are now short and PE waits between them for their loads. The pairs took 46.1 us, 46.9 said.
  - The price of a delay, 0.69 / 1.5 of itself, was too high for a short one, 1.4 us for 5.8: while DVE waits, POOL, too, runs alone and ends sooner (110.38 instead of 112.23), so more of DVE's passes take 0.69. Up to DVE's last output power the forecast of 2.1 was thus near the 1.4 by two errors against each other.
  - Of the 5.6 us in the table 5.2 lie between the first Toeplitz matmul and the GLU: 41.5 us in the kernel before, 46.7 after. Their cause is **open**. The old start-up took 44.6 at its second profile (experiment 3), so part is chance: the first GLU step came at 187.8 and 191.2 us in the two profiles of the old start-up, and at 191.6 to 194.0 in seven of the new one, so the start-up's price is about 3.6 us by their means, and two profiles of the old one don't tell this from 2.1. PE's wait for the third Toeplitz load was 4.1 and 5.4 us in the two old ones and 7.5 to 9.9 in all nine of the new ones whose units are not loaded early, with the same transfers in the same order. That this load shares its queue with the GLU's weights, and that PE waits for it, is shown by experiment 7; why it was slower is not.
- **Tail (-3.6).** Worth 2.8 in the kernel before and 5.3 in the changed one, so the size was right and the two profiles misled. The split was wrong: (b), 0.6, is not to be seen (experiment 2: 85.14 us in the stretch, with the moved half 84.5 to 85.3 apart from the 83.29 of after), and (a) carries all. That DVE sets the pace behind the first two units is confirmed (26.2 us both times), with ACT's split of 1.92 us on the same chain (experiment 10). Missed was the clock in head 6's third block: with the new counts PE waits up to 2.98 us there, with the old ones 1.08 in the same kernel (experiment 1), and the low clock behind it takes back about 2 us (23.5 us for the head, 21.1 with idle products, experiment 4).
- **The drain of the Trainium skill** (TensorEngine Tiling (Array Packing), Tiling Modes) doesn't show: in the rows of after the transposes begin at 92.04, where the unit of 91.07 ends, and eight records take 1.09 us in each of the seven groups that stand behind a unit at the high clock.
- **The sum.** Counted with the tail as the runs have it (2.8 to 5.3), the merge gained 1.9 us more than said and the start-up lost about 1.5 us more, so the total was hit in part by errors against each other.

## What to carry to other kernels

A stretch of small matmuls or a wait of PE has two prices: its own length, and the low clock behind it, here 0.57 over 4 us behind a reduction and 0.50 to 0.67 over 8 us behind a wait of 2.98 us. Look there before pricing either. Before you move or thin out cheap work, look at what wait it covers: it may be free where it stands. Where one engine works without a gap up to the end of a stage, look for what it does there that could be done in the idle time before, in memory that has just come free; that was worth 6 us here, the reordering on the engine that waits 3 to 5. Where two stages are compared, list what else stands on the engine that feeds them. And take two profiles of a stage whose clock varies.

## What was not expected of the hardware

- The length of the tail and its clock differ between profiles of the same code there: 83.3 to 85.3 us at 0.92 to 0.93 for the new tail in six profiles of the changed kernel and experiments 5 to 9; 84.65 at 0.92 and 88.47 at 0.86 for the old one, in the kernel before and in the changed one.
- DVE's passes of 128x4 elements take 0.17 us, and 1.2 us beside POOL's passes (894.26 in after), and where POOL paused for 1.1 us, PE's wait for DVE was 2.6 us shorter (experiment 3 against after).
- 16 turns of a row by one-element matmuls in four row groups, with a wait between the groups, took 4.4 us at a granted clock of 1.00, 6.3 and 6.4 at 0.63 and 0.62, and 7.6 at 0.50; in one group without waits they took 4.6 at 0.78 [rows 5].
- PE's wait for the third Toeplitz load varied by 1.3 us (4.1 and 5.4) in the old start-up and by 2.2 us (7.7 to 9.9) in seven profiles of the new one, with nothing changed in the start-up.
